# A decoder layer on one core: head logits issued two heads at a time in the row halves of the array, probabilities scaled before they are turned, values stationary

## The reference

```python
x = x + 0.5 * swiglu_ffn(x, ffn1_norm, ffn1_w_in, ffn1_w_out)
proj = rmsnorm(x, mix_norm) @ w_in            # u 256 | q 512 | k 512 | v 512 | qm 256
y_pool, new_buf = pool_mixer(u, pool_buf, pos, pool_w, pool_scale)
q = rotary(rmsnorm(q, q_norm), pos); k = rotary(rmsnorm(k, k_norm), pos)
y_moba = moba_attention(q, k_all, v_all, pos)  # 8 heads x 64
y_mem = mem_attention(qm, mk, mv)              # 4 heads x 64 over 256 memory tokens
x = x + concat(y_pool, y_moba, y_mem) @ w_out
x = x + 0.5 * swiglu_ffn(x, ffn2_norm, ffn2_w_in, ffn2_w_out)
```

## Time and profile before

| | us |
|---|---|
| median of 3 runs | 609.74 |
| runs | 608.29 to 612.21 |
| profiled execution | 607.76 |
| its span, first to last instruction | 606.0 |
| PE busy | 584.1 (96%) |
| DVE busy | 393.0 (65%) |
| ACT busy | 261.7 (43%) |

### The profile page before, as it was taken

The page is one execution under the profiler, slowest core; times in us unless marked ns, Lnnn a source line. Parts: engine busy times, 40 slices in busy tenths (PEclk is TensorE's granted clock), DMA queues, the critical chain, the costliest instruction groups (busy, mean ns, idle before and its releaser), DMA issues.

```text
span 606.0 us, 13646 instructions
## 1 busy us (share of the span) xinstructions
PE 584.1 (96%) x5168; PEld 536.8 (89%) x5168; DVE 393.0 (65%) x703; ACT 261.7 (43%) x408; POOL 16.1 (3%) x24
## 2 busy tenths in 40 slices
PE   7999999999999999999999798999999999989997
PEld 6999999999899997666667667989999999989996
DVE  3577677776698878698663621468767667674443
ACT  4843434434543346255264622474343434343331
POOL 1000000000000003000000000030000000000000
PEclk9899999999999999999999999999999999999999
DMA  9968777775677534996954889347655555566521
GB/s 278 279 195 244 230 225 221 214 239 176 209 236 268 203 128 153 345 380 215 380 210 141 273 297 354 99 131 209 174 174 173 173 173 174 180 208 201 173 69 72
DMA packets 132801, 128.41 MB, mean 212 GB/s; under 512 B 6560, under 2 KB 103927, under 8 KB 132751
## 3 DMA queue, kind: packets, MB, share of 16 engines
q1 hardware_dynamic: 132471, 127.76, 66.0%
q10 hardware_dynamic: 288, 0.08, 0.1%
HBM read 125.12 MB, written 2.83 MB: 211 GB/s over the span
## 4 chain that ended last, share of the span: by engine, by line
PE 83%; DVE 8%; issue 3%; ACT 3%; SPq 2%; DMA 1%; DVEq 0%; ACTq 0%; POOL 0%; POOLq 0%
PE banks L1385 23%; PE banks L1386 22%; PE banks L1387 22%; PE banks L1393 3%; DVE w_lo L919 2%; PE banks L1800 2%; PE banks L1719 2%; PE banks L1526 2%; PE banks L1738 2%; ACT w_hi L641 1%; SPq L445 1%; DVE kv L930 1%; PE banks L1566 1%; PE banks L1496 1%; SPq L456 1%
## 5 line engine op out<-in xcount | busy, mean ns | idle before, releaser
L919 DVE TENSOR_TENSOR w_lo<-raw,w_hi 128x1024 fp32r<-128x1024 f32 x160 | 195.8, 1230 | 111.7 <-ACT w_hi L641 111.1
L1385 PE MATMUL banks<-x_hi,w_hi 128*128 128x264 f32 x768 | 222.4, 290 | 6.9 <-DVE w_lo L919 3.7
L1386 PE MATMUL banks<-x_lo,w_hi 128*128 128x264 f32 x768 | 218.4, 284 | 0.0
L1387 PE MATMUL banks<-x_hi,w_lo 128*128 128x264 f32 x768 | 218.2, 284 | 0.0
L641 ACT ACTIVATE w_hi<-raw 128x1024 fp32r<-128x1024 f32 x160 | 163.6, 1050 | 78.6 <-PE banks L1387 70.0
L1385 PEld LDWEIGHTS banks<-x_hi,w_hi 128*128 128x128 f32 x768 | 145.3, 189 | 11.6 <-issue 5.8
L1386 PEld LDWEIGHTS banks<-x_lo,w_hi 128*128 128x128 f32 x768 | 145.4, 189 | 0.0
L1387 PEld LDWEIGHTS banks<-x_hi,w_lo 128*128 128x128 f32 x768 | 144.8, 188 | 0.0
L1385 PE MATMUL banks<-h_hi,w_hi 128*128 (+1 forms) x352 | 100.4, 285 | 2.3 <-DVE w_lo L919 2.2
L1387 PE MATMUL banks<-h_hi,w_lo 128*128 (+1 forms) x352 | 100.2, 285 | 0.0
L1386 PE MATMUL banks<-h_lo,w_hi 128*128 (+1 forms) x352 | 100.0, 284 | 0.0
(11 more groups left out here) (271 smaller groups left out, 523.4 us busy)
## 6 DMA issues: line engine op xcount, KB each, us to landing
...
kv<-in_cache_k SPq DMA_DIRECT2D x64, 256.0 KB, 5.0
kv<-in_cache_v SPq DMA_DIRECT2D x64, 256.0 KB, 4.8
...
raw<-in_w_in SPq DMA_DIRECT2D x8, 256.0 KB, 3.7
```

Source lines behind the costliest of these rows:

```text
L919: vec.tensor_tensor(w_lo[:, n % RING, :], raw[:, n % RING, :], w_hi[:, n % RING, :].bitcast(F32), ALU.subtract).then_inc(lo_ready, 1)
L1385: pe.matmul(out, lhs[0], rhs[0], start=start, stop=False)
L1386: pe.matmul(out, lhs[0], rhs[1], start=False, stop=False)
L1387: return pe.matmul(out, lhs[1], rhs[0], start=False, stop=stop)
```

## The change

- HA works on a pair of heads, one in partitions 0 to 63 of q and k and one in 64 to 127. Their matmuls alternate, so that neighbours use different row halves of the array. HA k now waits for `probT_ready` of the pair before.
- HV moves ahead of HB: DVE multiplies the probabilities of a head in SBUF by the reciprocal of their sum, two instructions a head, and HB waits for them (`p_scaled`).
- PV works on a pair too: v (64 columns) is the stationary operand and the turned probabilities move, so the result comes out turned, one head in each half of the output partitions, straight into the bank that HY splits. `y_tok`, and the turns of HY on PE, are gone.
- The memory logits of the samples (MK) use four groups of 32 output partitions in place of two; M and `rows_m` are 128 rows high in place of 64.
- ACT copies out four of the eight turned memory pages in place of two.
- The orders `EXTRA` (steps 11 to 15) and `TAIL` are rewritten; the first pass of MIX takes bank 4 last and waits for HY 2 only there.
- The `m_hi`, `m_lo` work of FFN 1 is in four blocks of two.
- The last pair of an FFN-in has a new order on DVE (`ffn_last`), and `ffn_out` waits for its first two units one by one.

```diff
-HY_BANKS, POOL_BANKS, MK_BANKS, QM_BANK = (7, 4, 4), (4, 5), (6, 4), 7
...
+HY_BANKS, POOL_BANKS, MK_BANKS, QM_BANK = (6, 7, 4), (4, 5), (6, 4), 7
+ACT_PAGES = (0, 2, 4, 6)
...
-            11: {2: [("T", 2)], 3: [("T", 3), ("ET", 4)], 4: [("S", 12), ("ET", 5), ("G", 28), ("G", 29)]},
-            12: {1: [("K", 6), ("HA", 0)], 2: [("HA", 1), ("HM", 0), ("HE", 0)], 3: [("HM", 1), ("HE", 1), ("WL", 13)],
-                 4: [("S", 13), ("G", 30), ("G", 31)]},
-            13: {0: [("HB", 0)], 1: [("HT", 0), ("HB", 1), ("WL", 14)], 2: [("HT", 1), ("K", 7)], 3: [("PV", (0,)), ("HV", (0,)), ("OWN", 0), ("A", 0)],
-                 4: [("S", 14), ("PV", (1,)), ("HV", (1,)), ("HA", 2), ("OWN", 1), ("WL", 15)]},
-            14: {1: [("HA", 3), ("HM", 2)], 2: [("HM", 3), ("HE", 2), ("A", 1)], 3: [("HE", 3), ("HB", 2)],
-                 4: [("S", 15), ("ES", 3), ("HT", 2), ("HB", 3), ("A", 2)]},
-            15: {0: [("HT", 3)], 1: [("PV", (2,)), ("X", 0), ("HV", (2,)), ("W", 16)], 2: [("PV", (3,)), ("HV", (3,)), ("A", 3), ("HA", 4)],
-                 3: [("ET", 6), ("HA", 5), ("NQ", 5), ("HM", 4), ("HE", 4)], 4: [("A", 4), ("HM", 5), ("NV", 5), ("ET", 7)]},
+            11: {2: [("T", 2)], 3: [("ET", 4), ("T", 3)], 4: [("S", 12), ("ET", 5), ("G", 28), ("G", 29)]},
+            12: {1: [("K", 6)], 2: [("HA", 0), ("HM", 0), ("HE", 0)], 3: [("HM", 1), ("HE", 1), ("WL", 13), ("HV", 0)],
+                 4: [("S", 13), ("HV", 1), ("G", 30), ("G", 31)]},
+            13: {1: [("HB", 0), ("HT", 0), ("WL", 14)], 2: [("HB", 1), ("HT", 1), ("K", 7)], 3: [("OWN", 0), ("A", 0), ("HA", 1), ("HM", 2)],
+                 4: [("S", 14), ("PV", 0), ("HM", 3), ("HE", 2), ("HE", 3), ("OWN", 1), ("WL", 15)]},
+            14: {1: [("HV", 2), ("HV", 3), ("A", 1), ("A", 2)], 3: [("HB", 2), ("HT", 2), ("HB", 3), ("HT", 3)],
+                 4: [("S", 15), ("ES", 3), ("HA", 2), ("HM", 4)]},
+            15: {0: [("A", 3), ("X", 0), ("HM", 5), ("HE", 4), ("HE", 5)], 1: [("PV", 1), ("W", 16)], 2: [("HV", 4), ("HV", 5)],
+                 3: [("ET", 6), ("NQ", 5), ("A", 4)], 4: [("HB", 4), ("HT", 4), ("HB", 5), ("HT", 5), ("NV", 5), ("ET", 7), ("A", 5)]},
         }
-        TAIL = ([("HE", 5), ("HB", 4), ("A", 5), ("T", 4), ("POOL", 0), ("HB", 5), ("HT", 4), ("V", 0), ("HT", 5), ("WL", 16), ("NQ", 6),
-                 ("PV", (4,)), ("HV", (4,)), ("W", 17), ("NV", 6), ("V", 1), ("PV", (5,)), ("HV", (5,)), ("POOL", 1), ("HA", 6), ("HA", 7), ("WL", 17),
-                 ("HM", 6), ("HM", 7), ("HE", 6), ("HE", 7), ("V", 2), ("ND", 5), ("ND", 6), ("HY", 0), ("HB", 6), ("HT", 6), ("HB", 7), ("HT", 7),
-                 ("NS", 5), ("NS", 6), ("W", 18), ("V", 3), ("YR", 0), ("PV", (6,)), ("HV", (6,)), ("PV", (7,)), ("HV", (7,)), ("QT", 1),
-                 ("HA", 8), ("HA", 9), ("WL", 18)] +
-                [("MG", b) for b in range(4)] + [("HM", 8), ("HM", 9), ("HE", 8), ("HE", 9), ("Y", 0)] + [("MG", b) for b in range(4, 8)] +
-                [("W", 19), ("HB", 8), ("HT", 8), ("V", 4), ("HB", 9), ("HT", 9), ("PV", (8,)), ("HV", (8,)), ("HA", 10), ("PV", (9,)), ("HV", (9,)),
-                 ("HA", 11), ("MK", 0), ("M", 0), ("WL", 19), ("HM", 10), ("HM", 11), ("HY", 1), ("HE", 10), ("HE", 11), ("V", 5), ("M", 1),
-                 ("HB", 10), ("HT", 10), ("M", 2), ("HB", 11), ("HT", 11), ("V", "mem"), ("YR", 1), ("PV", (10,)), ("HV", (10,)), ("PV", (11,)), ("HV", (11,)),
-                 ("V", 6), ("Y", 1), ("HY", 2), ("CAT", 0), ("MIX", 0), ("V", 7), ("YR", 2), ("MIX", 1), ("Y", 2), ("CAT", 1), ("MIX", 2),
-                 ("MX", 0), ("MX", 1), ("MX", 2), ("MIX", 3)])
+        TAIL = ([("HA", 3), ("T", 4), ("HM", 6), ("HM", 7), ("HE", 6), ("HE", 7), ("POOL", 0), ("PV", 2), ("HY", 0), ("V", 0), ("HV", 6), ("HV", 7),
+                 ("WL", 16), ("NQ", 6), ("W", 17), ("NV", 6), ("V", 1), ("HB", 6), ("HT", 6), ("HB", 7), ("HT", 7), ("POOL", 1), ("WL", 17),
+                 ("ND", 5), ("ND", 6), ("V", 2), ("PV", 3), ("NS", 5), ("NS", 6), ("HA", 4), ("HY", 1), ("W", 18),
+                 ("V", 3), ("YR", 0), ("WL", 18)] +
+                [("MG", b) for b in range(4)] + [("HM", 8), ("HM", 9), ("HE", 8), ("HE", 9), ("QT", 1)] + [("MG", b) for b in range(4, 8)] +
+                [("Y", 0), ("HV", 8), ("HV", 9), ("W", 19), ("V", 4), ("HB", 8), ("HT", 8), ("HB", 9), ("HT", 9), ("HA", 5), ("MK", 0), ("M", 0),
+                 ("HM", 10), ("HM", 11), ("PV", 4), ("HE", 10), ("HE", 11), ("WL", 19), ("V", 5), ("M", 1), ("HV", 10), ("HV", 11), ("M", 2),
+                 ("HB", 10), ("HT", 10), ("HB", 11), ("HT", 11), ("V", "mem"), ("YR", 1), ("PV", 5), ("HY", 2), ("V", 6), ("Y", 1), ("CAT", 0),
+                 ("MIX", 0), ("V", 7), ("YR", 2), ("MIX", 1), ("Y", 2), ("CAT", 1), ("MIX", 2), ("MX", 0), ("MX", 1), ("MX", 2), ("MIX", 3)])
...
-            for half in range(2):
-                for k in range(4 * half, 4 * half + 4):
+            for part in range(4):
+                for k in (2 * part, 2 * part + 1):
...
+                ffn_in_loop(0, M_TURN_AT + part, M_TURN_AT + part + 1 if part < 3 else HT // 2)
...
-                    if k >= 4:
-                        act.wait_ge(head_ready, k - 3)
...
+                if split_of is not None:
+                    split(split_of, 0, HT // 2 - 1)
...
+
+            def ffn_last(f):
+                n0, i = U_IN[f], HT // 2 - 1
+                split(n0 + 3, 0, i)
+                gate(f, i * 2, 0, i * 4 + n0)
+                up_hidden(f, i * 2, 0, i * 4 + n0)
+                split(n0 + 4, 0, i)
+                gate(f, i * 2 + 1, 1, i * 4 + (n0 + 2))
+                up_hidden(f, i * 2 + 1, 1, i * 4 + (n0 + 2), split_of=n0 + 5)
...
+                    vec.wait_ge(exp_done, 2 * k + 2)
+                    chain(vec.reciprocal(rc[:, k % 4], sm[:, k % 4]))
+                    for t in range(2):
+                        n = keys_of(k, t)[1]
+                        vec.tensor_scalar(prob_pair[:, k % 2, t, 0:n], prob_pair[:, k % 2, t, 0:n], rc[:, k % 4, t:t + 1], None, ALU.mult)\
+                            .then_inc(p_scaled, 1)
...
             def ffn_out(f):
                 n0 = U_OUT[f]
...
+                for k in range(2):
+                    pe.wait_ge(lo_ready, n0 + k + 1)
+                    pe.wait_ge(h_ready, HT * f + k + 1)
+                    for m in M_FIRST:
+                        if k == 0 and m == 4:
+                            pe.wait_ge(gu_free, HT * (f + 1))
+                        if f == 0 and k == 0 and m == 0:
+                            pe.wait_ge(mkv_ready, 2)
+                        mm = three(bank[m][:, 0:N], weights((n0 + k) % RING, m * P, (m + 1) * P), hidden(k), k == 0, False)
+                    mm.then_inc(w_used, 1)
...
+                for b in range(4):
+                    for half in range(2):
+                        keys = mem_page(4 * half + b).rearrange("p (t c k) -> p c t k", t=2, c=2)
+                        for hp in range(2):
+                            part = 32 * (2 * half + hp)
+                            mm = pe.matmul(bank[QM_BANK][part:part + 32, 0:NP], qm_cols[:, hp, 4 * half + b, :], keys[:, hp],
+                                           start=(b == 0), stop=(b == 3))
                 mm.then_inc(mk_used, 1)
...
+                        if k == 0 and m == HY_BANKS[2]:
+                            pe.wait_ge(hy_lo, 3)
...
+                    elif k < 5:
+                        pe.wait_ge(probT_ready, 2 * k)
...
+                        for u in (2 * k, 2 * k + 1):
+                            r = head_of(u)[1]
+                            c0, n = keys_of(u, t)
+                            mm = pe.matmul(bank[LANES[u]][:, c0:c0 + n], q_[r, hp, t * P:(t + 1) * P], k_[r, hp, 0:n], start=True, stop=not masked)
+                            if t and not masked:
+                                mm.then_inc(sc_ready, 1)
+                        for u in (2 * k, 2 * k + 1) if masked else ():
+                            c0, n = keys_of(u, t)
+                            mm = pe.matmul(bank[LANES[u]][:, c0 + n - P:c0 + n], ident_b[:], causal_b[:], start=False, stop=True)
+                            if t:
+                                mm.then_inc(sc_ready, 1)
...
-                    pe.wait_ge(exp_done, 2 * k + 2)
+                    pe.wait_ge(p_scaled, 2 * k + 2)
...
+                    masked = k < MH // 2
+                    v_, c0 = (vp, 2 * k * HD) if masked else (mem_kv, 256 + (2 * k - MH) * HD)
+                    at_ = k % 2 * NP
+                    for kt in range(2):
+                        for two in range(2):
+                            r, c1 = slice(HD * two, HD * two + HD), c0 + two * HD
+                            out, p0, p1 = (P, NP, 3 * P) if masked and kt else (0, kt * NP, kt * NP + NP)
+                            mm = pe.matmul(bank[HY_BANKS[k // 2]][r, at_ + out:at_ + NP], v_[:, kt, c1:c1 + HD], probT_pair[two][:, p0:p1],
+                                           start=(kt == 0), stop=(kt == 1))
```

(17 more changed lines are left out.)

133 lines of the change are left out of this document (38 added, 95 removed).

## The result

The changed kernel takes 601.06 us (median of 4 runs, 599.45 to 602.46) against 609.06 us for the kernel before on the same chip: a ratio of 0.9854, 95% interval 0.9823 to 0.9885. My forecast was 604.2, within 1% of before; it is 1.5% faster. The profiled execution took 600.45 us (span 598.7) against 607.76 (span 606.0). The case that came nearest is rival (a), 601.5.

The account below looks back on a forecast made before the run. PE, busy 96%, bounds the kernel, with SP and the DMAs as second chain in the mixer's tail. Terms -3.0 (mixer), -0.7 (FFN 1), -2.2 (FFN 2), +0.4 (clock) give -5.5: median 604.2 us, range 600.8 to 608.6.

Parts of the forecast that it names:

- within 1%: Whole kernel: time between 603.6 and 615.8 us, about what a measurement can't tell from no change; chance 0.54.
- rival (a): Mixer: heads' chain costs less, pairs at 1.3 us, V 0 ends at 323.0, V 7 starts at 372.0; 601.5 us, chance 0.22.
- V 0 to V 7: Mixer's tail: DMAs bound it, V 7 begins 49.0 us after V 0 ends instead of 53.8, so starts 3.0 earlier.
- FFN 1: 100 to 120 us: blocks of two pieces put work ahead of DVE's splits, -0.7 us (-0.3 to -1.1).
- from K 7 to the end of V 0: Mixer: added work and waits outweigh cheaper logits and PV, with K 7 +1.75 us; V 0 ends at 325.3.
- 1.7 us for a masked pair: Paired logits on PE: 1.7 us instead of 2.5, between 1.3 if all streaming overlaps and 2.4 if nothing does.
- The scaling: DVE: multiplying probabilities costs 0.75 us a head (0.5 to 0.9); K 7 comes 0.6 later (0 to 2).
- FFN 2's end: End of FFN 2 in: PE's wait for the second unit's w_lo goes whole, -2.2 us (-1.8 to -2.3).
- The clock: Whole kernel: +0.4 us for waits in which the clock may fall.
- case (d): PE: a clock that is low behind PE's waits; chance 0.13.
- Rival (b): Only the FFN ends count: V 0 at 328, V 7 at 377.0, mixer gives 0.3, rest 2.9; 606.5 us, chance 0.15.
- (c): Mixer: slower, heads' chain becomes the bound; with 3.5 us a pair V 0 ends at 334, median 612.6; chance 0.12.

Follow-up runs that it names:

- logits_serial: The changed kernel with the two heads of a pair's logits one after the other instead of in turns: 605.32 us, ratio 0.9944.
- pages_early: The changed kernel with SP's page-number reads for samples 4 and 5 moved ahead of the load of the memory keys: 596.26 us, ratio 0.9786.
- mk_two: The changed kernel with MK's 32 products in two groups of output partitions at a time instead of four: 601.63 us, ratio 0.9872.
- v6_first: The changed kernel with SP's load of v6 ahead of the w_out unit behind the memory values: 600.92 us, ratio 0.9866.
- mk_early: pages_early with HE 8 and HE 9 behind ACT's copies of memory pages, and HA 5 and MK ahead of HB 8 and HB 9: 597.31 us, ratio 0.9802.
- ffn_only: The kernel before with only the FFN edits (ffn_last, new waits in ffn_out, four blocks of two memory pieces): 603.36 us, ratio 0.9904.
- awake: mk_early with G 30, G 31 ahead of HV 0, HV 1, K 7 ahead of HB 0, HB 1, and 30 unused turns before V 6: 591.59 us, ratio 0.9701.

## Why the prediction was wrong

It named "within 1%" as likeliest, and the kernel came out 1.5% faster, inside the range. The step that failed is the place of V 0's end: the sum put it at 325.3 (323 to 328), and its own sign of being wrong was an end before 323; it was 321.6. The paths and the bounds were right (DVE at K 7, the DMAs from V 0 to V 7, the FFN ends), and terms of the sum were mis-sized. Of the difference, some 3.7 us, FFN 1 and an earlier start are 1.8 (the sum had 0.7 of FFN 1 in a term of its own, and none for the start); 1.2 stand ahead of K 6, where the sum had no term; and 0.6 are the term "from K 7 to the end of V 0" (+1.75 forecast, +1.12 measured).

- *K 7 to V 0.* I took 1.7 us for a masked pair and it is 1.37; with three pairs between K 7 and V 0 that is 1.0 us, of which other small terms took 0.4 back. The 1.7 rested on the 1.52 us of heads 8 and 9 as one meeting that saved 0.6. It was a full overlap (1.13 us for one head or two) that began 0.4 us late, behind HV 7 (see logits_serial), so the row held no price for a meeting, and alternating is not what a memory pair's overlap needs (1.14 us one behind the other, 1.13 in turns).
- *The change of tile shape.* The sum has no term for it. The changed kernel's rows show the product behind one of 512 columns some 0.09 us later where its shape is another (0.32 against 0.23). The four changes fewer a pair may be part of what 1.7 missed, some 0.4 us by that estimate; PV, whose products have a shape of their own now (`128*64`), takes 0.80 us where I had 0.85.
- *Ahead of K 6* (-1.17) didn't hold PE's wait for ACT's copy of vp (1.3 us), though the trace had it, and I costed the exchange of T 3 and ET 4 at nothing. Of the 1.2 us the order is 0.5; the rest is the landing of a unit, which varies by 2 us between executions; that part is luck.
- *The scaling* was costed rightly: 0.66 us a head for 0.75, and K 7 came 0.89 later behind K 6, for 0.6. HA 3 waits 1.0 for HT 5; I had laid out 1.6, 0.9 of them new.
- *V 0 to V 7.* DMA-bound, as argued: 4.07 us gained, 4.8 forecast, and 337 GB/s in 331 to 371.3 us for the 345 taken. SP's wait for MK went and PE's waits for pages came. SP's wait for V 0 should have been longer than 15.0 us and is 14.6. I took the 9.4 us ahead of v4 as given ("unchanged"); pages_early shows that 4.9 of them were to be had. That PE's savings between V 0 and V 7 don't arrive: mk_two and v6_first agree.
- *FFN 1* gave 1.4, not 0.7. The busy time of 100 to 120 us grew by 1.02, all that PE lacked there; I had counted on two thirds, and where the other 0.4 lay I haven't found. *FFN 2's end* gave 2.3 for 2.2.
- *The clock.* The sum has +0.4 for it, a guess of mine that no run shows. In the profiled execution of the changed kernel V "mem" took 3.53 us instead of 1.86, which moved nothing that shows, since v6 landed later; in the four runs named under mk_early, which have its order there, V 7 began 0.9 to 1.3 us after its last page behind a V 6 of 3.2 to 3.5 us, and that may be so in the executions of the changed kernel that have no profile. That is case (d) of my chances, at about 1 us. V 7 to FFN 2 took 1.0 more for another reason: a unit of `w_in` landed at 389.98, and ACT's split, DVE's and the eight residual chunks stand behind it. In ten of the twelve experiments this stretch is 0.2 to 0.9 longer than before, in ffn_only and awake not; what sets it I haven't tried.
- *The levels.* My sum gave 602.3 for the profiled execution, which was 600.45. The 7.3 us between the two profiled executions are less than what the ratio says, 0.0146 x 609 = 8.9 (7.0 to 10.8); the profiled one of before lay 1.3 us under its median, that of the changed kernel 0.6.

The three terms that were too small for the gain (0.7 of FFN 1, 1.2 ahead of K 6, 0.6 behind it) add up to 2.5 us, the two too large (0.7 from V 0, 0.6 from V 7) to 1.3; 0.6 more came from the start, the end and FFN 2. That is the 1.8 between 5.5 and 7.3. Rival (a) had V 0 at 323.0 and V 7 at 372.0, measured 321.6 and 371.4. Its pair of 1.3 us was near (1.37), but its other reason was not: K 7 waits 1.3 us and HA 3 1.0. That its sum came nearest is in part luck, FFN 1 and a unit that landed early. Rival (b) is refuted by the mixer's part of 4.1 us up to V 7, and (c) by V 0, which stands 158.9 us behind FFN 1 out, as before.
